# Attention stage: projections, transposes and early output products on two 128x64 column tiles of TensorE

## The reference, cut to what matters

```python
qkv = proj[..., D_A_COLS:].reshape(b, t, 3, H_B, N_B)
q, k, v = qkv[:, :, 0], qkv[:, :, 1], qkv[:, :, 2]
...
s_loc = jnp.einsum('brqhn,brkhn->bhrqk', qr, kg).astype(jnp.float32) * ATTN_SCALE
...
p = jax.nn.softmax(jnp.concatenate([s_loc, s_ctx], axis=-1), axis=-1).astype(v.dtype)
o = (jnp.einsum('bhrqk,brkhn->brqhn', p[..., :n_loc], vg)
     + jnp.einsum('bhrql,blhn->brqhn', p[..., n_loc:], ctx_v))
...
x = x + gt1 * jnp.einsum('bte,ed->btd', jnp.concatenate([ya, yb], axis=-1), w_out)
```

## Time and profile before

| | us |
|---|---|
| median of 3 runs | 3619.27 |
| lowest and highest | 3618.79, 3622.28 |
| span of the profiled execution, first to last instruction | 3612.2 |
| attention stage in it, from 918.8 to 1316.0 | 397.2 |
| TensorE busy in the whole span | 3408.1 |

### The profile page before, as it was taken

How to read it: one execution, slowest core, us unless ns; L and a number is a source line. 1 busy time by engine, 2 the same in 40 slices (tenths; PEclk the granted TensorE clock), 3 DMA queues, 4 the chain that set the end, 5 groups by cost and what they waited for, 6 DMA issues and landing times.

```text
span 3612.2 us, 83473 instructions
## 1 busy us (share of the span) xinstructions
PE 3408.1 (94%) x37698; PEld 2976.7 (82%) x37698; DVE 1102.5 (31%) x2770; ACT 735.5 (20%) x1815; POOL 385.0 (11%) x536
## 2 busy tenths in 40 slices
PE   7989898898999997499999999999999999999998
PEld 3575767667455544499999999999999999999998
DVE  4566666575344444411111111111111111111113
ACT  3435344343244433000000000000000000000002
POOL 0141514233211000000000000000000100000001
PEclk9999999999999998799999999999999999999999
DMA  8200000000311122697777778787778878777775
GB/s 353 71 5 9 18 10 17 5 20 5 102 32 26 43 77 93 226 362 264 281 269 275 268 274 275 264 288 258 272 276 280 275 267 283 263 281 269 274 264 185
DMA packets 500080, 666.46 MB, mean 185 GB/s; under 512 B 31598, under 2 KB 438406, under 8 KB 496654
## 3 DMA queue, kind: packets, MB, share of 16 engines
q1 hardware_dynamic: 494030, 641.74, 50.5%
q0 software_dynamic: 5520, 19.34, 2.0%
q10 hardware_dynamic: 176, 0.05, 0.0%
HBM read 631.68 MB, written 28.30 MB: 183 GB/s over the span
## 4 chain that ended last, share of the span: by engine, by line
PE 58%; SPq 1%; DMA 0%; DVE 0%; ACT 0%; issue 0%; DVEq 0%
PE banks L2465 38%; PE banks L2477 19%; PE banks L2488 0%; PE banks L2423 0%; DMA e_wd<-in_e_down 0%; SPq L2335 0%; SPq L2339 0%; SPq L2336 0%; SPq L2334 0%; ACT e_wd L2558 0%; PE banks L2447 0%; DVE e_ye L2632 0%; DVE e_wu L2718 0%; DVE e_wu L2661 0%; DVE e_xe L2707 0%
## 5 line engine op out<-in xcount | busy, mean ns | idle before, releaser
L2465 PE MATMUL banks<-e_xT,e_wg 128*128 128x144 f32 x5632 | 747.9, 287 | 1.9 <-DVE e_xT L2598 1.6
L2477 PE MATMUL banks<-e_hid,e_wd 128*128 128x144 f32 x5632 | 748.1, 287 | 0.0
L2465 PE MATMUL banks<-e_xT,e_wu 128*128 128x144 f32 x5632 | 747.6, 287 | 0.0
L2465 PEld LDWEIGHTS banks<-e_xT,e_wg 128*128 128x128 f32 x5632 | 713.8, 191 | 2.4 <-DMA e_wd<-in_e_down 2.3
L2465 PEld LDWEIGHTS banks<-e_xT,e_wu 128*128 128x128 f32 x5632 | 713.8, 191 | 0.0
L2477 PEld LDWEIGHTS banks<-e_hid,e_wd 128*128 128x128 f32 x5632 | 711.1, 191 | 0.0
L2608 DVE TENSOR_TENSOR e_tm<-banks,e_sg 128x144 f32<-128x144 f32 x352 | 108.3, 308 | 1790.3 <-ACT e_sg L2544 1790.3
L2544 ACT ACTIVATE e_sg<-banks 128x144 f32<-128x144 f32 x352 | 102.1, 290 | 1937.6 <-PE banks L2465 1937.6
L606 PE MATMUL banks<-hT_x,wblk 128*128 128x512 f32 (+1 forms) x624 | 212.7, 496 | 0.0
L606 PEld LDWEIGHTS banks<-hT_x,wblk 128*128 128x128 f32 x624 | 102.8, 192 | 100.1 <-issue 98.5
L1398 DVE TENSOR_TENSOR r_TW<-r_TW,banks 128x256 f32<-128x256 f32 (+1 forms) x360 | 129.3, 392 | 78.3 <-PE banks L830 74.1
(11 more groups left out here) (383 smaller groups left out, 3572.0 us busy)
## 6 DMA issues: line engine op xcount, KB each, us to landing
e_wg<-in_e_gate SPq DMA_DIRECT2D x176, 1024.0 KB, 5.2
e_wu<-in_e_up SPq DMA_DIRECT2D x176, 1024.0 KB, 7.5
e_wd<-in_e_down SPq DMA_DIRECT2D x176, 1024.0 KB, 10.2
h_wmod<-in_w_mod SPq DMA_DIRECT2D x24, 1024.0 KB, 15.2
wblk<-in_w_in SPq DMA_DIRECT2D x22, 512.0 KB, 21.5
h_x<-in_x_sample SPq DMA_DIRECT2D x8, 512.0 KB, 6.8
wo<-in_w_out SPq DMA_DIRECT2D x2, 2048.0 KB, 12.0
scratch_ffn<-hT_x SPq DMA_DIRECT2D x8, 512.0 KB, 5.2
```

The source lines that it names most:

```text
L2465: last = nc.tensor.matmul(bank[6 + b % 2][:, j * TOK:(j + 1) * TOK], w[s][:, k, f], xT[e % 2][:, k, :], start=(k == 0), stop=(k == KD - 1))
L2477: last = nc.tensor.matmul(bank[k // PER_BANK][:, c:c + TOK], wd[s][:, b % DUO, k * P:(k + 1) * P], hid[:, b % 2, :], start=(b == 0 and k % ...
```

## The change

Every call that used the whole array in this stage now uses two column tiles: `HS` holds the slices 0:64 and 64:128, each call becomes two, one for the first and one for the second 64 columns of the stationary operand, with the same moving operand, and each writes its own 64 partitions of the same bank. The transposes become ordinary matmuls against the identity, in steps of 64 columns; a block of 64 columns takes one such call.

```diff
                     for kc in chunks:
-                        last = nc.tensor.matmul(piece_bank(p, n)[:, 0:m], wblk[b][:, kc, :], K.hT[:, kc, at:at + m],
-                                                start=(kc == 0), stop=(kc == KD - 1))
+                        for hs in HS:
+                            last = nc.tensor.matmul(piece_bank(p, n)[hs, 0:m], wblk[b][:, kc, hs], K.hT[:, kc, at:at + m],
+                                                    start=(kc == 0), stop=(kc == KD - 1))
...
-                        last = nc.tensor.matmul(bank[7][:, :], y, K.wo[:, kc, j * 512:(j + 1) * 512],
-                                                start=(kc == 0), stop=(kc == KD - 1))
+                        for hs in HS:
+                            last = nc.tensor.matmul(bank[7][hs, :], y[:, hs], K.wo[:, kc, j * 512:(j + 1) * 512],
+                                                    start=(kc == 0), stop=(kc == KD - 1))
...
+                def across(out, src):
+
+                    n = src.shape[1]
+                    for at in range(0, n, HN):
+                        last = nc.tensor.matmul(out[at:at + HN, :], src[:, at:at + HN], K.ident[:, :], start=True, stop=True)
+                    return last
...
-                        nc.tensor.transpose(out[:, 0:P], k[p % 2][:, NS:NT], K.ident[:, :]).then_inc(t_ps, 1)
+                        across(out[:, 0:P], k[p % 2][:, NS:NT]).then_inc(t_ps, 1)
...
-                        last = nc.tensor.transpose(out[:, i * P:(i + 1) * P], v[:, t * P:(t + 1) * P], K.ident[:, :])
+                        last = across(out[:, i * P:(i + 1) * P], v[:, t * P:(t + 1) * P])
...
-                        last = nc.tensor.transpose(out[:, P:2 * P], ckrow[:, :], K.ident[:, :])
+                        last = across(out[:, P:2 * P], ckrow[:, :])
...
-                        last = nc.tensor.transpose(bank[4 + b // 4][0:n, (b % 4) * P:(b % 4 + 1) * P],
-                                                   pr[U % 2][h][:, at:at + n], K.ident[:, :])
+                        last = across(bank[4 + b // 4][0:n, (b % 4) * P:(b % 4 + 1) * P], pr[U % 2][h][:, at:at + n])
```

## The result

| | before | after |
|---|---|---|
| median of 5 runs, us | 3619.27 | 3650.18 |
| lowest to highest | 3615.11 to 3622.28 | 3648.29 to 3656.75 |
| span of the profiled execution | 3612.2 | 3646.5 |

The ratio is 1.009, with a 95% interval of 1.0078 to 1.0102: the change costs 28 to 37 us. The forecast was 3651.3. The three runs of the kernel before that stand ahead of the prediction are among the five.

What follows compares the result with a forecast made beforehand. TensorE was taken to bound the kernel. Transposes +44.3 us, changes of shape -3.9, -1.8 and -0.9, hidden time -5.7: +32.0, forecast 3651.3 us, 0.9% slower; range 3641 to 3664, rivals left out.

Steps and rivals of the forecast that it cites:

- What bounds the stage: Attention stage: TensorE is busiest, 377.86 of 397.2 us, so time added to its stream lengthens the program nearly one for one.
- wide units: The 26 attention units with a wide piece of projection work, where TensorE's stream has no hole and nothing hides added time.
- Column tiles cost nothing, with 512 columns too: Projections and output products: a pair of 512-column instructions, one per tile, runs side by side in 0.429 us, costing nothing more.
- A block of 128 columns at 0.219 us: Transposes: a block becomes four instructions, 0.219 us instead of 0.109; 372 blocks add 40.9 us.
- The 64-column blocks at +0.105: Transposes: 32 blocks of 64 columns get two instructions on the same tile, +0.105 us each, +3.4 us together.
- Changes of shape: TensorE entering another instruction shape: 0.15 us into column tiles, 0.2 into the whole array; gains of 3.9, 1.8 and 0.9 us.
- Cover: Part of the transposes' loss hidden while TensorE waits for DVE before weighted sums, outside units with a wide piece: -5.7 us.
- narrow unit: Attention unit with a narrow piece, where weighted sums wait for DVE's eviction of block 4, hiding part of the longer transposes.
- Unit 2: Attention unit whose wait for DVE was to hide all 0.655 us plus about 0.15 of head 0's: 3 x 0.8 = 2.4 us.
- unit 5: Attention unit whose wait for DVE was to hide 0.5 of the 0.655 us added to head 1's transposes: 3 x 0.5 = 1.5.
- the unit without a piece: Attention unit carrying no projection piece; the added transpose time of both heads was to be hidden, 1.1 us.
- the rival built on it: Transposes: ordinary matmuls cost four times the transpose mode, a block 0.436 us, +132 us, about 3739; chance 0.01.

Runs made afterwards that it cites:

- the calls alone: The kernel before with projections and early output products on two column tiles, transposes left as they were: 3627.71 us against 3616.63, ratio 1.0034.

## Why the prediction was right

- **What bounds the stage: right.** TensorE's added time shows one for one in the wide units, 6.99 us for 6.98.
- **Column tiles cost nothing, with 512 columns too: right.** It was the step with no row of before behind it. 3.48 us for a portion of eight wide pairs and 1.72 for one of four leave no room for a weight load to show, and the calls alone show it without the dearer transposes.
- **A block of 128 columns at 0.219 us: right.** 1,376 instructions, 1.09 us for five blocks. The 64-column blocks at +0.105: right too. From its first portion to the first one of the next unit a wide unit with twelve blocks, two of them of 64 columns, took 1089.91 - 1078.47 = 11.44 us and takes 1103.17 - 1090.63 = 12.54, +1.10; one with ten took 1118.62 - 1108.79 = 9.83 and takes 1134.90 - 1124.19 = 10.71, +0.88. That leaves 0.11 for each of the two.
- **Changes of shape: right in kind.** Into the column tiles 0.15 as forecast. Out of them it depends on what follows: 0.2 for ordinary matmuls on the whole array (0.34 for the two changes, less 0.15), 0.15 for transposes (0.31 less 0.15). The 26 entries into the weighted sums have gone (1.72 for 1.81 and the 0.06 behind it).
- **Cover: right in place, its size too large.** This is the term of the sum that was off: 4.6 us and not 5.7. The wait before the weighted sums says what is hidden in a narrow unit. Unit 2 before and after, then unit 5 before and after:

```profile
1075.05 1.09 PE L1745 MATMUL banks<-t_pt,t_vtok 128*64 128x128 f32 x16 [0.90 <-ACT t_pt L1815]
...
1086.98 1.09 PE L1753 MATMUL banks<-t_pt,t_vtok 128*64 128x128 f32 x16 [0.25 <-ACT t_pt L1823]
...
1105.64 1.09 PE L1745 MATMUL banks<-t_pt,t_vtok 128*64 128x128 f32 x16 [0.63 <-ACT t_pt L1815]
...
1120.85 1.09 PE L1753 MATMUL banks<-t_pt,t_vtok 128*64 128x128 f32 x16 [0.25 <-ACT t_pt L1823]
```

  0.65 us went in unit 2 where 0.8 was forecast, 0.4 in unit 5 where 0.5 was; the unit without a piece hid 0.9 of 1.1. In unit 5 DVE now comes late as well, since it waits for head 0's blocks,

```profile
1117.97 0.28 DVE L1914 COPY t_pt<-banks 64x128 f32<-64x128 f32 x1 [0.57 <-PE banks L1669]
```

  which it hadn't done before the change, where it came straight from its maximum.
- **The sum.** With the cover at 4.6 the terms give +33.1; behind the clock's falls +30.7 was measured, to which the 2.3 us of the 21 blocks ahead of the first weighted sum belong, less a little for shapes: 33.0. That it came out at +30.9 in the medians and +34.3 in the spans lies within what runs differ by (of the 34.3, 3.0 us had arisen before the stage began and 1.8 behind it, in stages that the change leaves alone). That the medians meet the forecast's +32.0 within about 1 us is thus in part luck; the clock at the start of the stage, which the forecast did not consider, moves an execution by some 3 us.
- **The factor of four.** The Trainium skill gives it for the transpose mode in FP32 (page "TensorE: Matmul & The Clock Gate", section "Terms"). Here a block in transpose mode costs half of one by ordinary matmuls (0.109 us for 0.219), not a quarter. The trace of the changed kernel decides this as that of before did, and the rival built on it is out.

## What to carry to other kernels

In float32 and with 128 or 512 columns moving, as here, a whole-array call of 128 stationary columns gains nothing from being split into two column tiles and loses nothing either; what the split buys is one shape with its neighbours, worth 0.15 us a change on a full stream here. It must not be paid with an instruction that has to give up a cheaper mode: a float32 transpose of 128x128 costs 0.109 us as a transpose and 0.219 as two tiles against an identity, so that a head of five blocks loses 0.55 to save at most 0.31, the price of the two changes around it when all else is on tiles. Count the instructions a call becomes (one, two, four) in the groups by form before trusting that a rewrite is the same work.

## What the runs showed of the hardware that was not expected

- A pair's cycle in the stage repeats to 0.01 us in 95 between two executions, while the program's medians of the same kernel moved from 3619.27 to 3616.63 and 3610.41 us between three sets of runs, the last two of which the record puts on different chips. For a change inside one stage, a cycle inside it is the finer measure.
- The sixth block's two instructions seem to occupy one column tile while the other goes on. In the changed kernel an instruction of the next portion starts before the block's last one (1117.56 and 1117.66 in a narrow unit), though the program has it behind. The trace doesn't name the tiles; that the early one is on the second tile is inferred:

```profile
1117.23 0.59 PE L1669 MATMUL banks<-ident,t_p 128*64 128x128 f32 x6
1117.56 0.32 PE L1640 MATMUL banks<-hT_x,wblk 128*64 128x128 f32 x1
1117.66 0.27 PE L1669 MATMUL banks<-ident,t_p 128*64 128x128 f32 x1
```
